# A two-block hybrid network on one core: the end of each layer's output product in parts, later rounding of gated tiles, and one moved key/value product

## The reference

```python
for l in range(DEPTH):                       # DEPTH = 2
    a, g, zc, q, k, v, za, qi, ki, wi = jnp.split(h @ w_in[l], IN_SPLITS, axis=-1)
    y_conv = conformer_conv_branch(a, g, zc, conv_w[l], ...)   # 31 taps, layer norm, silu gates
    score = sum over 8 index heads of relu(qi . ki) * wi       # keep the 132 best keys per row
    y_attn = softmax attention (8 heads of 64) over the kept keys * silu(za)
    y = concatenate([y_conv, y_attn]) @ w_out[l]               # 528 x 1024 by 1024 x 1024
    h = layer_norm(alpha * h + y, post_ln_g[l], post_ln_b[l])
# second block
z = rmsnorm(x) @ w_in_2                      # q, k, v, gate_a, u_in, v_in, gate_b, g_merge
attn = block_attention(axial_rope(q), axial_rope(k), v) * silu(gate_a)
gm = gelu(u_in) * spatial_mix(layernorm(gelu(v_in))) * silu(gate_b)
out = rmsnorm(x + (g0 * (attn @ w_proj_attn) + g1 * (gm @ w_proj_gmlp)) @ w_out_2)
```

## Time and profile before

| what | value |
|---|---|
| median of 3 runs | 1014.51 us (1014.0 to 1015.2) |
| the profiled execution, its own time | 1014.03 us |
| its span in the trace | 1012.2 us |
| mean granted clock of PE | 0.991 |
| PE busy | 982.5 us, 97% of the span |
| DVE, ACT, POOL busy | 668.4, 559.6, 232.4 us |

### The profile page before, as it was taken

How to read it: one execution, slowest core, us unless ns; L and a number is a source line. 1 busy time by engine, 2 the same in 40 slices (tenths; PEclk the granted TensorE clock), 3 DMA queues, 4 the chain that set the end, 5 groups by cost and what they waited for, 6 DMA issues and landing times.

```text
span 1012.2 us, 15815 instructions
## 1 busy us (share of the span) xinstructions
PE 982.5 (97%) x6084; PEld 819.3 (81%) x6084; DVE 668.4 (66%) x1444; ACT 559.6 (55%) x920; POOL 232.4 (23%) x254
## 2 busy tenths in 40 slices
PE   8999999999999999999999999999999999999997
PEld 7888998986677988888878677888888788888886
DVE  4899999988673499999988756638522333333432
ACT  6685891655343568598165424544646566564442
POOL 0110671125212401077111511624101000000001
PEclk9999999999999999999999899999999999999999
DMA  8876885752001577487475300478777536366662
GB/s 299 198 183 169 214 195 135 174 118 85 1 1 66 143 186 175 121 192 183 125 170 122 118 21 1 169 172 199 180 215 198 116 87 162 88 162 129 173 160 83
DMA packets 23962, 143.92 MB, mean 142 GB/s; under 512 B 2880, under 2 KB 3648, under 8 KB 8272
## 3 DMA queue, kind: packets, MB, share of 16 engines
q0 software_dynamic: 8496, 60.36, 32.2%
q1 hardware_dynamic: 15392, 82.55, 23.0%
HBM read 140.81 MB, written 2.10 MB: 141 GB/s over the span
## 4 chain that ended last, share of the span: by engine, by line
PE 80%; DVE 10%; ACT 3%; issue 2%; POOL 2%; DMA 2%; SPq 1%; POOLq 0%; DVEq 0%; ACTq 0%
PE psum_B L1404 20%; PE psum_A L1404 13%; PE psum_B L1438 8%; PE psum_A L1438 8%; PE psum_A L1600 6%; DVE conv_acc L1918 4%; PE psum_C L1480 2%; PE psum_C L1404 2%; PE psum_A L1815 2%; PE psum_B L1815 2%; DMA w_raw<-in_weights 2%; PE psum_B L1544 2%; POOL w_lo L1184 2%; PE psum_B L1802 2%; PE psum_A L1516 2%
## 5 line engine op out<-in xcount | busy, mean ns | idle before, releaser
L1191 POOL DMA_DIRECT2D w_lo<-in_weights x59 | 52.0, 881 | 545.9 <-ACT w_lo L728 493.7
L1918 DVE SCALAR_TENSOR_TENSOR conv_acc<-u,vec,conv_acc 128x528 f32<-128x528 f32 (+1 forms) x240 | 172.4, 756 | 3.2
L1404 PE MATMUL psum_B<-x_hi,w_hi 128*128 128x272 f32 (+3 forms) x456 | 138.1, 337 | 0.5 <-ACT shifted L785 0.3
L1404 PE MATMUL psum_B<-x_hi,w_lo 128*128 128x272 f32 (+3 forms) x456 | 135.4, 331 | 0.0
L1404 PE MATMUL psum_B<-x_lo,w_hi 128*128 128x272 f32 (+3 forms) x456 | 135.3, 331 | 0.0
L727 ACT ACTIVATE w_hi<-w_raw 128x2048 fp32r<-128x2048 f32 (+2 forms) x73 | 113.4, 1553 | 25.8 <-DMA w_raw<-in_weights 25.3
L728 ACT ACTIVATE w_lo<-w_raw 128x2048 fp32r<-128x2048 f32 (+2 forms) x73 | 112.7, 1545 | 0.0
L1404 PE MATMUL psum_A<-x_hi,w_hi 128*128 128x272 f32 (+3 forms) x368 | 100.1, 315 | 0.8 <-DMA w_lo<-in_weights 0.4
L1404 PE MATMUL psum_A<-x_lo,w_hi 128*128 128x272 f32 (+3 forms) x368 | 98.1, 309 | 0.0
L1404 PE MATMUL psum_A<-x_hi,w_lo 128*128 128x272 f32 (+3 forms) x368 | 97.9, 309 | 0.0
L1404 PEld LDWEIGHTS psum_B<-x_hi,w_hi 128*128 128x128 f32 (+1 forms) x456 | 79.0, 187 | 10.0 <-issue 1.7
(11 more groups left out here) (409 smaller groups left out, 2294.9 us busy)
## 6 DMA issues: line engine op xcount, KB each, us to landing
w_raw<-in_weights SPq DMA_DIRECT2D x65, 1024.0 KB, 5.0
w_lo<-in_weights POOLq DMA_DIRECT2D x57, 1024.0 KB, 8.3
x_first<-in_x_t SPq DMA_DIRECT2D x8, 264.0 KB, 6.3
h<-in_x SPq DMA_DIRECT2D x1, 2048.0 KB, 9.8
out<-h SPq DMA_DIRECT2D x4, 512.0 KB, 2.6
w_raw<-in_weights SPq DMA_DIRECT2D x2, 512.0 KB, 7.6
post_ln_g<-in_post_ln_g SPq DMA_DIRECT2D x2, 512.0 KB, 4.6
post_ln_b<-in_post_ln_b SPq DMA_DIRECT2D x2, 512.0 KB, 6.3
```

Source lines behind the costliest of these rows:

```text
L1191: pool.dma_start(wlo[n % RING][:, 0:width], io["weights"][n, :, 0:width], accum_op=ALU.add) \
L1404: mm = pe.matmul(ps[0:cols, i, o:o + b - a], w[wp][:, kt, at:at + cols], x[xp][:, kt, a:b], start=(kt == 0 and wp + xp == 0), stop=(kt == ...
L1918: got = dve.scalar_tensor_tensor(dst, src, w, dst, ALU.mult, ALU.add)
```

## The change

- The last output product of each layer's items (n=1, tile 3) is made in two parts of 12 matmuls, set at two items, and in layer 1 the conv half for tile 4 is cut into two parts of 6 as well (`LAST_OUTPUT_AT`).
- In layer 0's tail PE makes the last product of tile 4 before it turns row tile 3; DVE does the post norm of tile 3 around the last gate, and POOL's second subtraction of a weight block stands behind the deviation of tile 4. In layer 1's tail DVE makes the inputs of the second block's tiles 1 and 2 before the last gate, and ACT rounds tile 1 before it splits weights.
- `KV_AND_Q`: the key/value product of the last tile comes after three half products of q instead of one, and the turn of row tile 4 after the first of them.
- ACT: `y_hi` is taken out of `woven` and done in `gated(i-2)` and `gated(i-1)`, which stand after the copy of the transposed probabilities of item i. The gated tiles are rounded one pair later in ACT's list.

```diff
@@ -254,22 +254,27 @@
 
 OUTPUT_AT = {
     0: ((17, 0, 0, "A"), (19, 0, 1, "C"), (22, 1, 0, "A"), (25, 1, 1, "B"), (27, 0, 2, "A"), (29, 1, 2, "A"),
-        (34, 0, 3, "A"), (36, 1, 3, "A")),
-    1: ((17, 0, 1, "A"), (19, 0, 2, "B"), (21, 1, 1, "A"), (23, 1, 2, "A"), (26, 0, 3, "A"), (28, 1, 3, "A")),
+        (34, 0, 3, "A")),
+    1: ((17, 0, 1, "A"), (19, 0, 2, "B"), (21, 1, 1, "A"), (23, 1, 2, "A"), (26, 0, 3, "A")),
 }
 
 
 META_AT = ((14, "attn"), (14, "conv"))
-POST_AT = {0: ((0, 26), (1, 28), (2, 32), (3, 38)), 1: ((1, 22), (2, 26), (3, 30))}
-
-OUTPUT_CONV_AT = {0: 38, 1: 30}
+POST_AT = {0: ((0, 26), (1, 28), (2, 32)), 1: ((1, 22), (2, 26), (3, 30))}
+
+
+LAST_OUTPUT_AT = {
+    0: ((36, "wo conv", 0, 0, 4), (37, "wo part", 0, 1, 3, "C", 0, 4), (38, "wo part", 1, 1, 3, "C", 0, 4)),
+    1: ((28, "wo part", 0, 1, 3, "A", 0, 4), (29, "wo part", 1, 1, 3, "A", 0, 4), (30, "wo conv", 0, 0, 2),
+        (31, "wo conv", 0, 2, 4)),
+}
 OUTPUT_BANK = (("A", 1), ("B", 1))
 
 
 INPUT_BANK = {0: ("D", "C", "D", "C", "D"), 1: (None, "D", "C", "D", "C")}
 
 
-KV_AND_Q = (("kv", 0), ("kv", 1), ("kv", 2), ("q", 0, 0), ("kv", 3), ("q", 1, 0), ("q", 2, 0), ("q", 3, 0),
+KV_AND_Q = (("kv", 0), ("kv", 1), ("kv", 2), ("q", 0, 0), ("q", 1, 0), ("q", 2, 0), ("kv", 3), ("q", 3, 0),
             ("q", 0, 1), ("q", 1, 1), ("q", 2, 1), ("q", 3, 1))
 KV_BANK = (("A", 0), ("B", 0), ("A", 1), ("B", 1))
 Q_BANK = (("A", 0), ("B", 0), ("A", 1), ("D", 0))
@@ -344,6 +349,7 @@
     for i, part, t, buf in OUTPUT_AT[l]:
         todo["pe"][i].append(("wo", part, t, buf))
         todo["dve"][i + 1].append(("residual", part, t))
+    todo["dve"][39 if l == 0 else 29].append(("residual", 1, 3))
     for t, i in POST_AT[l]:
         todo["dve"][i].append(("aggregate", t))
         todo["pool"][i].append(("deviation", "post", t))
@@ -351,7 +357,11 @@
         if l == DEPTH - 1:
             todo["act"][i + 1].append(("square", t))
             todo["pool"][i + 1].append(("input", t))
-    todo["pe"][OUTPUT_CONV_AT[l]].append(("wo conv", 0))
+    for i, *op in LAST_OUTPUT_AT[l]:
+        todo["pe"][i].append(tuple(op))
+    if l == 0:
+        todo["dve"][39].append(("aggregate", 3))
+        todo["pool"][39].append(("deviation", "post", 3))
     if l == 0:
         todo["pool"][12].append(("clear", 0))
         for i, part in META_AT:
@@ -473,7 +483,7 @@
         K_AT = where[0]
         k = sb("k", [P, CT, L])
         xt0 = sb("x_first", [P, KD, L], at=Q_AT)
-        hn = [sb("h_normed0", [P, D], at=K_AT + 4 * D), sb("h_normed1", [P, D], at=where[0])]
+        hn = [sb(f"h_normed{i}", [P, D], at=K_AT + 4 * D * i) for i in range(2)]
         v = sb("v", [P, 5, DC])
         XS_AT = where[0]
         xs = [sb(f"shifted{i}", [P, L]) for i in range(4)]
@@ -995,7 +1005,10 @@
                             pair_meta((l, part), meta_pair[1], slice(0, CT) if part == "conv" else slice(CT, KD), META)
                         elif op[0] == "tanh":
                             conv_tanh(l, op[1])
-                        elif op[0] == "hi":
+
+                def gated(i):
+                    for op in todo[i]:
+                        if op[0] == "hi":
                             y_hi(l, *op[1:])
 
                 def gates(i):
@@ -1005,6 +1018,9 @@
 
                 for i in range(0, n, 2):
                     take_probs_t(l, i)
+                    if i:
+                        gated(i - 2)
+                        gated(i - 1)
                     if i + 2 < n:
                         exps(l, i + 2)
                         exps(l, i + 3)
@@ -1017,6 +1033,8 @@
                     woven(i + 1)
                 after = NUMBER[(l + 1, "a" if l < DEPTH - 1 else "kv", 0)]
                 y_hi(l, "attn", 4)
+                if l == DEPTH - 1:
+                    x_hi(l, 1)
                 split_hi(after)
                 if l < DEPTH - 1:
                     x_hi(l, 0)
@@ -1027,7 +1045,6 @@
                     split_hi(after + 2)
                     x_hi(l, 4)
                 else:
-                    x_hi(l, 1)
                     x_hi(l, 2)
                     split_hi(after + 1)
                     x_hi(l, 3)
@@ -1302,8 +1319,14 @@
 
                 after = NUMBER[(l + 1, "a" if l < DEPTH - 1 else "kv", 0)]
                 subtract_hi(after)
-                subtract_hi(after + 1)
-                ln_deviation((l, "post", 4), 4, P)
+                if l < DEPTH - 1:
+                    subtract_hi(after + 1, (0,))
+                    ln_deviation((l, "post", 4), 4, P)
+                    pool.wait_ge(normed.sem, normed.at((l, "x", 4)))
+                    subtract_hi(after + 1, (1,))
+                else:
+                    subtract_hi(after + 1)
+                    ln_deviation((l, "post", 4), 4, P)
                 split_lo(after + 2)
                 if l == DEPTH - 1:
                     input_deviation(4)
@@ -1584,14 +1607,14 @@
                     mm = pe.transpose(ps[:, kt // 4, kt % 4 * P:kt % 4 * P + n], src[:, kt * P:kt * P + P], ident[0:n, 0:n])
                 mm.then_inc(psum_full.mark(use), 1)
 
-            def output_half(l, n, half, t, ps):
+            def output_half(l, n, half, t, ps, kks=range(4)):
 
                 part = ("conv", "attn")[half]
                 pe.wait_ge(part_lo.sem, part_lo.at((l, part, t)))
                 w = [block_[:, :].rearrange("p (k c) -> p k c", k=4) for block_ in weights(NUMBER[(l, "wo", n, half)])]
                 if t == 0:
                     pe.wait_ge(meta_paired.sem, meta_paired.at((l, part)))
-                for kk in range(4):
+                for kk in kks:
                     kt = half * 4 + kk
                     if t == 0:
                         mm = meta_product(ps, meta_pair[1], kt, w[0][:, kk, :], w[1][:, kk, :])
@@ -1607,10 +1630,20 @@
                 output_half(l, n, 0, t, ps)
                 output_half(l, n, 1, t, ps).then_inc(psum_full.mark(use), 1)
 
-            def output_conv(l, n):
+            def output_part(l, half, n, t, buf, first, last):
+
+                use = (l, "wo", n, t)
+                ps = (bank[buf][:, 1:2, :] if half else claim(use, buf, (1,)))[:, 0, :]
+                mm = output_half(l, n, half, t, ps, range(first, last))
+                if half and last == 4:
+                    mm.then_inc(psum_full.mark(use), 1)
+
+            def output_conv(l, n, first=0, last=4):
                 buf, at = OUTPUT_BANK[n]
-                ps = claim((l, "wo", n, 4), buf, (at,))[:, 0, :]
-                output_half(l, n, 0, 4, ps).then_inc(psum_full.mark((l, "wo", n, 4, "conv")), 1)
+                ps = (bank[buf][:, at:at + 1, :] if first else claim((l, "wo", n, 4), buf, (at,)))[:, 0, :]
+                mm = output_half(l, n, 0, 4, ps, range(first, last))
+                if last == 4:
+                    mm.then_inc(psum_full.mark((l, "wo", n, 4, "conv")), 1)
 
             def output_attn(l, n):
                 buf, at = OUTPUT_BANK[n]
@@ -1705,6 +1738,8 @@
                             turn_conv_back(l, *op[1:])
                         elif op[0] == "wo":
                             output_rows(l, *op[1:])
+                        elif op[0] == "wo part":
+                            output_part(l, *op[1:])
                         else:
                             output_conv(l, *op[1:])
@@ -1731,8 +1766,10 @@
                 output_attn(l, 0)
                 if l < DEPTH - 1:
                     turn_rows(l, 2)
+                    output_attn(l, 1)
                 turn_rows(l, 3)
-                output_attn(l, 1)
+                if l == DEPTH - 1:
+                    output_attn(l, 1)
 
 
             SPARE = "B", (1,)
@@ -1835,10 +1872,10 @@
                     x_ready(1, t + 1)
                     buf, at = KV_BANK[t]
                     rows((2, "kv", t), NUMBER[(2, "kv", 0)], x, META + P * t, 1, 2 * P, 0, KD, banks=(buf, (at,)))
-                    if t == 2:
-                        turn_rows(1, 4)
                 else:
                     query_half(t, *half)
+                    if (t, *half) == (0, 0):
+                        turn_rows(1, 4)
             turn["AB"] = 1
             for name in ("vin", "u", "gb"):
                 for t in range(4):
@@ -2124,7 +2161,7 @@
                 dve.bn_aggr(meanvar[0:n, t, :], stats[0:n, t, :, :].rearrange("p a b -> p (a b)")) \
                     .then_inc(stats_made.mark((l, "post", t)), 1)
 
-            def post_norm(l, t):
+            def post_norm(l, t, between=None):
 
                 n = SIZE[t]
                 step = (l, "post", t)
@@ -2133,6 +2170,8 @@
                 dve.wait_ge(ln_loaded, 32 * (l + 1))
                 dve.scalar_tensor_tensor(row, row, meanvar[0:n, t, 0:1], ln_g[0:n, :], ALU.subtract, ALU.mult) \
                     .then_inc(dve_step.mark((l, "gain", t)), 1)
+                if between:
+                    between()
                 dve.wait_ge(dve_step.sem, dve_step.at((l, "gain", t)))
```

(25 more changed lines are left out.)

## The result

The changed kernel takes 1035.85 us (median of 4 runs, 1033.31 to 1038.84) against 1014.66 us: a ratio of 1.0219, 95% interval 1.0206 to 1.0233, or 22 us slower. The forecast was 1023 with a range up to 1029. The sign was right and the size was not. The profiled execution took 1038.84 us, of which 1037.0 are the span, at a mean granted clock of 0.982 (before: 0.991).

What follows compares the result with a forecast made beforehand. PE, busy 97% of the span, was taken as the bound. Ends -4.6, late rounding +8.1, load +3.4 and clock +1.5 sum to +8.4 us on 1014.03, or 1022.4; forecast 1023, range 1014.5 to 1029.

Steps and rivals of the forecast that it cites:

- The wait of 1.24 us for a copy in layer 1: Layer 1 attention: PE's wait for ACT's copy goes, since the copy no longer waits for a `y_part`.
- The late rounding: Attention items, both layers: rounding behind the copy makes `x_lo`, deviations and subtractions late; +8.1 us (5.3 to 10.4).
- the five places: Late rounding's places: layer 0 +0.7, +2.2 and +1.5 us; layer 1 +0.4 and +3.3 us.
- The cover of 3.7 us: Layer 0, item 20: slack of POOL's output-weight subtraction before; once late, PE waits +1.5 us for that block.
- The turn back of tile 4: Layer 0, after item 18's copy: late rounding, `x_lo`, deviation and bias delay this turn; +2.2 us (1.6 to 2.9).
- The clock: PE's lower clock level behind new waits of about 3 us and longer turn waits; +1.5 us (0 to +4.5).
- a chance of 0.13: Rival that the clock falls more: two or three more slow stretches, +4.5 to +7 us, 1027 to 1030; chance 0.13.
- The load of vin1: First product of v_in: later key/value product delays SP's load, split and DMA; PE stalls +3.4 us (0.9 to 4.9).
- The ends: Ends of both layers: six short PE waits covered by products placed there; -4.6 us, weak end -2.5.
- that one, at the turn of tile 4: Layer 1's end: the wait at 660.37 goes, with a half product of q ahead of the turn; -1.0 us.
- The rival "faster": Copy ahead of rounding gains, and POOL and DVE catch up; 1010 to 1012 us, chance 0.14.

Runs made afterwards that it cites:

- round_alone: Kernel before with one edit alone: gated tiles rounded behind the next copy of probabilities, at all items; ratio 1.0174, +17.6 us.
- late_18_layer0: Kernel before with only item 18's rounding in layer 0 (conv tile 3) late, and with it POOL's 4.7 us subtraction; ratio 1.0040, +4.1 us.
- late_16_layer1: Kernel before with only the roundings of items 16 and 17 of layer 1 (conv tile 3, attention tile 2) late; ratio 1.0043, +4.4 us.
- kv_late: Kernel before with the last key/value product behind three half products of q, turn of row tile 4 behind the first; ratio 1.0072, +7.3 us.
- ends_kv_turn: Kernel before with the change's ends, tile 4's turn behind the first half product of q, last key/value product behind the second, vin1 by DMA; ratio 0.9998.
- kv_one_less: Kernel before with the last key/value product behind two half products of q, tile 4's turn behind the first; ratio 1.0026, +2.6 us.
- ends_alone: Kernel before with split last output products and the tails' new order, without late rounding or new `KV_AND_Q`; ratio 0.9975, -2.5 us.

## Why the forecast was right or wrong

**Most places were right.** The waits of PE of 1 us and more at the turns back, for the output block, for `x_lo` and at the load of vin1 had been named, with their chains. The two waits for masks (0.49, 1.23) had not. The wait of 1.24 us for a copy in layer 1 was said to go and became 1.58: that copy still stands behind a tanh that waits for a `y_part` (ACT waits 2.81 us for it), and this `y_part` is later.

**The late rounding, +8.1, measured +17.6.** The step that failed is the sum over the five places, at each of which I priced the chain that PE waits for and nothing that the moved work on POOL does to others. By place the forecast was 1.1, 2.2, 1.5 and 3.3, and the runs 2.5, 3.6, 4.1 and 4.4. By waits alone it was 4.4 in layer 0 and 3.7 in layer 1, and the trace of `round_alone` has 7.3 and 3.4.
- What a late subtraction does to DVE. "The cover of 3.7 us" was slack of PE's need alone. Moving 4.7 us of POOL's work by 6 us (256.34 in `late_18_layer0`, 250.29 before) puts it beside other work of DVE, and that was priced at nothing; it is the largest error (waits of 3.8 us for 1.5). The wait for the block itself came out at 1.00, below the forecast; the masks and what follows them are the rest.
- The turn back of tile 4 measured 3.2 us, or 2.8 more than the 0.34 that PE waited there before. This is inside the stated 1.6 to 2.9, but at its upper end. I took +2.2 from between "DVE free" and "DVE blocked", though the same bias beside POOL stood in a row at 1.75 us. In the change it took 1.74. The Trainium skill, SBUF — State Buffer, section "Who interferes with whom", says that a DVE instruction with two SBUF inputs contends with a GpSimd instruction that reads SBUF, that the shared ports are an exclusive lock, and that the order of issue decides who blocks. The rows agree: 0.75 alone, 1.74 beside an `x_lo` that had started 0.07 us earlier, 2.83 beside the first half of a subtraction that had started 0.12 us earlier. The blocked case should have been the value and not the upper end.
- The clock. In layer 0 PE's busy time grew by 4.5 us in `round_alone`, in stretches at or near the lower level behind the waits (behind the turns back and behind the masks). It is not so at every place: `late_16_layer1` stays at 1.00 behind 3.11 us.

**The clock, +1.5, is the second mis-sized term.** It was a single sum for two waits of about 3 us. The mean clock went from 0.991 to 0.982 and PE's busy time grew by 10.0 us. The Trainium skill, TensorE: Matmul & The Clock Gate, section "HAM oscillation — how this bites in real kernels", says that work behind a wait for data starts at the lower level. I gave that a chance of 0.13 since the trace before had no wait of 3 us; the trace after has three, each with a granted clock of 0.50 to 0.64 behind it, and `late_16_layer1` has one without. By that rule the sum would have been 3 us more, still short of 22.

**The load of vin1, +3.4, measured a wait of 6.84 us and +7.3 us in all.** The chain was right, and the correction was wrong in sign. I cut the stall from 4.9 to 3.4 because the raw load might be faster at a quieter time. SP issued it at 686.86 and ACT started on it at 695.68, 8.8 us, about what it had been. Then POOL issued the DMA of `w_lo` at 699.76, and PE started at 710.77, 11.0 us instead of 8.1. The listing of DMA issues from 676 to 706 us shows both kinds at work:

```profile
w_raw<-in_weights SPq DMA_DIRECT2D x3, 1024.0 KB, 10.4
w_lo<-in_weights POOLq DMA_DIRECT2D x2, 1024.0 KB, 9.9
```

The next two raw loads wait for the last product of q, whose time the new order hardly moves, so a later `w_lo` meets them. They follow its issue by this much, and it lands after this long:

| kernel | raw loads behind the issue of `w_lo` | landing of `w_lo` |
|---|---|---|
| the change | 0.7 us | 11.0 us |
| kv_late | 0.8 | 10.4 |
| ends_kv_turn | 3.4 | 8.6 |
| kv_one_less | 3.9 | 8.3 |
| before | 5.9 | 8.1 |

I had named the next load in a clause and priced the opposite. That those loads slow `w_lo` is read from these five traces, not tried alone.

**The ends, -4.6, measured -2.5 alone.** Five waits went, and in the change the sixth too. I priced that one, at the turn of tile 4, as covered by the half product of q. With the moved turn this holds, and a wait of 0.46 us for a copy on ACT stands ahead of it; without it, as in `ends_alone`, the wait grows from 0.97 to 2.65. So the term was about right in kind; the five alone were forecast at -3.6. Measured with everything else that slows DVE and PE in the change, the ends' gain cannot be read apart.

**The rival "faster"** rested on POOL catching up. It had no room: PE's products of 24 matmuls stood ahead of the copies as the order showed.

## What to carry to other kernels

Price a late producer by what its work now lies beside, not only by who waits for it: a subtraction of 4.7 us moved by 6 us cost more through DVE than through the wait for its result. Where waits of some us are added to a busy PE, give the half speed behind them a price of its own, up to the length of the slow stretch over two for each; here the waits alone were 14.8 of the 24.8 us by which the profiled span grew. A load that a matrix product releases has a chain (load, split, second DMA) whose length is to be held against PE's time to its use in the new order, with the neighbours' loads at their new times too; shortening the chain took the same new order from a loss of 7.3 us to one of 2.1, and with the product one half product earlier and the new ends it is part of a gain of 6.2.

## What was not expected of the hardware

- The granted clock falls behind short waits too, if not always. In the change 1.94 us of waiting, in a stretch with small transposes and scores, is followed by 4.1 us at 0.50. In `late_18_layer0` waits of 1.01 and 0.49 us leave it at 1.00 and one of 1.23 is followed by 0.58. In `kv_one_less` a wait of 1.78 us between large products leaves it at 1.00, and so does one of 3.11 us in `late_16_layer1`, which in the change is followed by 0.64. So the length of the wait alone does not decide it.
- Two stretches of before at the lower clock, at 517 and at 571 us (the earlier trace rows is the second), were absent or shorter in the profiles of several kernels that run the same instructions there; in `late_18_layer0` PE was busy 1.4 us less at each (at the first, a wait of 1.14 us for a mask took most of it back). So a single profile's shift holds up to 2 or 3 us that are the clock's and no edit's, which is one reason why the shifts of a profile and the ratios of five rounds differ by some us.
- A DVE operation with one large and one column input (`exps` times `prob_rsums`) also waited beside POOL's subtraction, 2.27 us in place of 0.36, and 1.25 in place of 0.43 in layer 1.
